# Order and rows of the matmuls in a chunked RWKV-7 recurrence inside a two-block kernel

## What is computed

```python
def rwkv7_recurrence(r, decay, k, v, a_vec, b_vec):
    """S_t = S_{t-1} diag(w_t) + (S_{t-1} a_t) b_t^T + v_t k_t^T ;  y_t = S_t r_t."""
    def step(state, inp):
        r_t, w_t, k_t, v_t, a_t, b_t = inp
        sa = jnp.einsum('bhvk,bhk->bhv', state, a_t)
        state = (state * w_t[:, :, None, :] + sa[..., None] * b_t[:, :, None, :]
                 + v_t[..., None] * k_t[:, :, None, :])
        return state, jnp.einsum('bhvk,bhk->bhv', state, r_t)
    ...
```

## Time and profile before

| what | value |
|---|---|
| median of three runs | 1117.88 us |
| lowest, highest | 1114.72, 1118.47 us |
| profiled execution, its own time | 1117.52 us |
| its span in the trace | 1115.7 us |
| PE busy | 1088.8 us (98% of the span) |
| DVE, ACT, POOL busy | 670.3, 448.1, 35.6 us |
| matmul records | 8212 |

### The profile page before, as it was taken

The page is one execution under the profiler, slowest core; times in us unless marked ns, Lnnn a source line. Parts: engine busy times, 40 slices in busy tenths (PEclk is TensorE's granted clock), DMA queues, the critical chain, the costliest instruction groups (busy, mean ns, idle before and its releaser), DMA issues.

```text
span 1115.7 us, 19112 instructions
## 1 busy us (share of the span) xinstructions
PE 1088.8 (98%) x8212; PEld 896.2 (80%) x8212; DVE 670.3 (60%) x848; ACT 448.1 (40%) x573; POOL 35.6 (3%) x29
## 2 busy tenths in 40 slices
PE   9999999999998999999999999999999999999997
PEld 8999998999987669999998999989899753434343
DVE  6488777789554666777775573277559552222123
ACT  6333334864522244333335332267584521211112
POOL 0000000000430000000003000000000000000000
PEclk9999999999978999999999999999999999999999
DMA  9977756354200248598873353332356979999994
GB/s 333 390 257 238 251 188 206 119 175 148 90 2 2 76 140 314 190 337 295 306 265 114 96 184 110 108 118 104 114 192 264 375 319 402 422 410 419 422 418 201
DMA packets 121012, 254.29 MB, mean 228 GB/s; under 512 B 6241, under 2 KB 91505, under 8 KB 109426
## 3 DMA queue, kind: packets, MB, share of 16 engines
q1 hardware_dynamic: 119890, 250.54, 61.6%
q10 hardware_dynamic: 1056, 2.79, 0.8%
HBM read 252.25 MB, written 1.06 MB: 227 GB/s over the span
## 4 chain that ended last, share of the span: by engine, by line
PE 89%; DVE 6%; ACT 4%; issue 1%; DMA 0%; SPq 0%; ACTq 0%; DVEq 0%
PE ps L825 53%; PE ps L772 33%; ACT arena L1563 2%; DVE ring_r L2130 1%; ACT arena_r L1563 1%; DVE ring_r L2263 1%; PE ps L1308 1%; DVE arena L2451 1%; DVE arena L2317 1%; DMA x<-in_x 0%; DVE arena L2332 0%; PE ps L793 0%; ACT gb_r L1563 0%; PE ps L1513 0%; PE ps L781 0%
## 5 line engine op out<-in xcount | busy, mean ns | idle before, releaser
L825 PE MATMUL ps<-hall_r,arena_r 128*128 128x256 f32 x1632 | 299.6, 281 | 0.0
L825 PE MATMUL ps<-arena_r 128*128 128x256 f32 (+1 forms) x1216 | 284.4, 323 | 0.0
L2130 DVE TENSOR_TENSOR ring_r<-ring,arena_r 128x2048 fp32r<-128x2048 f32 x88 | 203.1, 2312 | 109.1 <-ACT arena_r L1563 106.6
L825 PEld LDWEIGHTS ps<-hall_r,arena_r 128*128 128x128 f32 x1632 | 252.8, 188 | 1.2 <-issue 0.3
L1563 ACT ACTIVATE arena_r<-ring 128x2048 fp32r<-128x2048 f32 (+1 forms) x101 | 191.1, 1899 | 150.3 <-PE ps L825 139.9
L825 PE MATMUL ps<-hall_r,ring_r 128*128 128x256 f32 x816 | 227.9, 279 | 0.0
L825 PEld LDWEIGHTS ps<-arena_r 128*128 128x128 f32 x1216 | 202.7, 188 | 18.9 <-issue 0.7
L772 PE MATMUL ps<-arena 64*64 64x32 f32 (+7 forms) x1944 | 195.8, 331 | 11.2 <-ACT arena L1563 5.0
L1563 ACT ACTIVATE arena<-ps 128x512 f32<-128x512 f32 (+3 forms) x136 | 80.4, 605 | 312.6 <-PE ps L825 186.2
L772 PEld LDWEIGHTS ps<-arena 128*64 128x64 f32 (+3 forms) x1944 | 117.8, 154 | 71.1 <-issue 58.6
L825 PEld LDWEIGHTS ps<-hall_r,ring_r 128*128 128x128 f32 x816 | 154.9, 190 | 0.9
(11 more groups left out here) (273 smaller groups left out, 1137.8 us busy)
## 6 DMA issues: line engine op xcount, KB each, us to landing
ring<-in_w_in SPq DMA_DIRECT2D x35, 1024.0 KB, 5.2
arena<-in_w_exp_down SPq DMA_DIRECT2D x32, 1024.0 KB, 11.8
ring<-in_ffn_up SPq DMA_DIRECT2D x22, 1024.0 KB, 5.3
ring<-in_ffn_down SPq DMA_DIRECT2D x22, 1024.0 KB, 5.0
ring<-in_ffn_gate SPq DMA_DIRECT2D x21, 1024.0 KB, 5.7
arena<-in_w_mod SPq DMA_DIRECT2D x18, 1024.0 KB, 9.3
arena<-in_w_exp_up SPq DMA_DIRECT2D x16, 1024.0 KB, 14.5
ring<-in_w_exp_gate SPq DMA_DIRECT2D x16, 1024.0 KB, 11.4
```

Source lines behind the costliest of these rows:

```text
L825: m = pe.matmul(out_, w[i], h[j], start=start and i + j == 0, stop=stop and j == 1, skip_group_check=group)
L2130: tt(lo(n), slot(n), hi(n), ALU.subtract).then_inc(S("w_lo"), 1)
```

## The change

Before, all products of a chunk stood together behind the waits. Now those that need only v stand ahead of the waits, in functions of their own: the right side's (`rec_rhs_v`) for the next chunk behind y of this one, the state's (`rec_state_v`) between the right side and u, y's (`rec_y_v`) between u and the wait for its copy. The first right side stands behind `inv_sums(5)`, ahead of the head sums and of `inv_update(5)`. Every product that takes its rows from a chunk (all but those with the state) contracts over that chunk's 64 rows (`rec_rows(c)`), so that the zeros aren't needed: v is kept once (`v_t`, two copies in place of four multiplications), and `u_zero` goes. The products with the state keep their 128 rows. The state's sums move from bank 4 to bank 7. ACT copies the first right side ahead of the attention's output and root, and DVE scales the attention's output behind each chunk's state; it waits for the last of these before the means of y. `keep_running` is defined and not called.

```diff
@@ -174,10 +174,10 @@
                         "dve_mix": [("cum", 2), ("kk_raw", 4), ("bonus_prod", 1), ("kk_unit", 1), ("b_bar", 1), ("k_bar", 1),
-                        ("arz", 4), ("bonus_v", 1), ("q_ready", 1), ("v_tok", 4), ("gram_b_masked", 4),
+                        ("arz", 4), ("bonus_v", 1), ("q_ready", 1), ("v_tok", 2), ("gram_b_masked", 4),
                         ("kn", 1)],
             "pool_all": [("c_zero", 2), ("selectors", 2), ("reset_ones", 1), ("reset_mask", 1), ("inv_0", 4),
-                         ("level_a", 5), ("u_zero", 1), ("gates_biased", 4), ("w_zero", 1)],
+                         ("level_a", 5), ("gates_biased", 4), ("w_zero", 1)],
             "pool_rec": [("rec_masked", 3), ("x_zero", 1)],
                          ("logits_kept_a", 1), ("final_a", 1)],
@@ -429,7 +429,7 @@
         kk, sq, kf = tiles(13), tiles(14), tiles(15)
         arz = A(16, 4096).rearrange("p (q k c j n) -> p q k c j n", q=2, k=4, c=NCH, j=2)
         b_bar, k_bar, bonus = tiles(20), tiles(21), tiles(22)
-        vz = A(0, 2048).rearrange("p (q t n) -> p q t n", q=2, t=TT)
+        v_t = A(0).rearrange("p (t n) -> p t n", t=TT)
         b_tok = A(13).rearrange("p (t n) -> p t n", t=TT)
         k_tok = A(10).rearrange("p (t n) -> p t n", t=TT)
         ab_t, rb_t, ak_t, rk_t = (A(j).rearrange("p (i n) -> p i n", n=CH) for j in (6, 7, 8, 9))
@@ -744,9 +744,6 @@
             for level in range(3, 6):
                 level_mask(level)
 
-            pool.wait_ge(*W("inv_x", 5))
-            pool.memset(A(20, 2048), 0.0).then_inc(S("u_zero"), 1)
-
             pool.wait_ge(*W("mod_kept", 3))
             pool.wait_ge(*W("gate_bias", 64))
             for j in range(4):
@@ -1038,7 +1035,7 @@
             pe.wait_ge(*W("b_bar", 1))
             by_token(b_bar, 4, "b_turned")
             project(11, True)
-            pe.wait_ge(*W("v_tok", 4))
+            pe.wait_ge(*W("v_tok", 2))
             pe.wait_ge(*W("k_sq", 1))
             four(6, lambda o, k: mm(o, head_mean, sb_sq_k[:, k, :]), "k_ms")
             project(12, True)
@@ -1136,6 +1133,59 @@
                         else:
                             m = mm(out_, inv_x[half, i, :], blocks_of(inv_tt[half, i, :], level, 1))
                 m.then_inc(S("inv_t"), 1)
+
+            def rec_rows(c):
+                return slice((c % 2) * CH, (c % 2 + 1) * CH)
+
+            def rec_rhs_v(c):
+                for h in range(8):
+                    m = mm(ps[rec_rows(c), 0, h * CH:(h + 1) * CH], ak_t[rec_rows(c), 8 * (c // 2) + h, :],
+                           v_t[rec_rows(c), c // 2, h * HD:(h + 1) * HD], start=h == 0, stop=c == 0, group=True)
+                if c == 0:
+                    m.then_inc(S("rec_rhs"), 1)
+
+            def rec_rhs_state(c):
+                for h in range(8):
+                    m = mm(ps[rec_rows(c), 0, h * CH:(h + 1) * CH], arz[:, h % 2, h // 2, c, 0, :],
+                           state[:, c % 2, h // 2, :], start=False, group=True)
+                m.then_inc(S("rec_rhs"), 1)
+
+            def rec_state_v(c):
+                for h in range(8):
+                    o = ps[(h % 2) * HD:(h % 2 + 1) * HD, 7, (h // 2) * HD:(h // 2 + 1) * HD]
+                    mm(o, k_tok[rec_rows(c), c // 2, h * HD:(h + 1) * HD],
+                       v_t[rec_rows(c), c // 2, h * HD:(h + 1) * HD], start=h < 2, stop=False, group=True)
+
+            def rec_state_u(c):
+                for h in range(8):
+                    o = ps[(h % 2) * HD:(h % 2 + 1) * HD, 7, (h // 2) * HD:(h // 2 + 1) * HD]
+                    m = mm(o, b_tok[rec_rows(c), c // 2, h * HD:(h + 1) * HD],
+                           u_z[rec_rows(c), c % 2, h * HD:(h + 1) * HD], start=False, group=True)
+                m.then_inc(S("rec_state"), 1)
+
+            def rec_y_at(c, h):
+                return ps[(h % 2) * HD:(h % 2 + 1) * HD, 2 + c % 2, (h // 2) * CH:(h // 2 + 1) * CH]
+
+            def rec_y_v(c):
+                if c >= 2:
+                    pe.wait_ge(*W("y_kept", c - 1))
+                for h in range(8):
+                    mm(rec_y_at(c, h), v_t[rec_rows(c), c // 2, h * HD:(h + 1) * HD],
+                       rk_t[rec_rows(c), 8 * (c // 2) + h, :], start=h < 2, stop=False, group=True)
+
+            def rec_y_u(c):
+                for h in range(8):
+                    m = mm(rec_y_at(c, h), u_z[rec_rows(c), c % 2, h * HD:(h + 1) * HD],
+                           rb_t[rec_rows(c), 8 * (c // 2) + h, :], start=False, stop=c == 0, group=True)
+                if c:
+                    for h in range(8):
+                        m = mm(rec_y_at(c, h), state[:, c % 2, h // 2, :], arz[:, h % 2, h // 2, c, 1, :],
+                               start=False, group=True)
+                m.then_inc(S("rec_y"), 1)
+
+            def keep_running():
+                for i in range(2):
+                    mm(ps[:, 7, 0:256], zeros[:, 0:P], zeros)
 
             for p in range(4):
                 sb_scores(p)
@@ -1155,49 +1205,36 @@
             sb_values(1)
             inv_sums(5)
             pe.wait_ge(*W("sb_expo", 4))
+            pe.wait_ge(*W("rec_masked", 3))
+            rec_rhs_v(0)
             pe.wait_ge(*W("sbo_sq", 2))
             four(4, lambda o, k: mm(o, head_mean, sq[:, k, :]), "sbo_ms")
             inv_update(5)
 
 
-            pe.wait_ge(*W("rec_masked", 3))
             for c in range(NCH):
-                t, base = c // 2, (c % 2) * CH
-                rows_ = slice(base, base + CH)
-                pe.wait_ge(*W("tt_added", 5))
                 if c:
                     pe.wait_ge(*W("state", c))
-                for h in range(8):
-                    o = ps[rows_, 0, h * CH:(h + 1) * CH]
-                    if c:
-                        mm(o, arz[:, h % 2, h // 2, c, 0, :], state[:, c % 2, h // 2, :], stop=False)
-                    m = mm(o, ak_t[:, 8 * t + h, :], vz[:, c % 2, t, h * HD:(h + 1) * HD], start=c == 0)
-                m.then_inc(S("rec_rhs"), 1)
+                    rec_rhs_state(c)
+                if c < NCH - 1:
+                    rec_state_v(c)
+                if c == 0:
+                    pe.wait_ge(*W("sb_kept", 1))
+                    rec_y_v(c)
+                    pe.wait_ge(*W("tt_added", 5))
                 pe.wait_ge(*W("rhs_kept", c + 1))
                 for h in range(8):
-                    m = mm(ps[rows_, 1, h * CH:(h + 1) * CH], inv_tt[:, 8 * t + h, :],
-                           rhs_z[:, c % 2, h * HD:(h + 1) * HD])
+                    m = mm(ps[rec_rows(c), 1, h * CH:(h + 1) * CH], inv_tt[rec_rows(c), 8 * (c // 2) + h, :],
+                           rhs_z[rec_rows(c), c % 2, h * HD:(h + 1) * HD])
                 m.then_inc(S("rec_u"), 1)
+                if c:
+                    rec_y_v(c)
                 pe.wait_ge(*W("u_kept", c + 1))
-                if c == 0:
-                    pe.wait_ge(*W("sb_kept", 1))
-                    pe.wait_ge(*W("sbo_root", 1))
                 if c < NCH - 1:
-                    for h in range(8):
-                        o = ps[(h % 2) * HD:(h % 2 + 1) * HD, 4, (h // 2) * HD:(h // 2 + 1) * HD]
-                        mm(o, b_tok[:, t, h * HD:(h + 1) * HD], u_z[:, c % 2, h * HD:(h + 1) * HD], stop=False)
-                        m = mm(o, k_tok[:, t, h * HD:(h + 1) * HD], vz[:, c % 2, t, h * HD:(h + 1) * HD],
-                               start=False)
-                    m.then_inc(S("rec_state"), 1)
-                if c >= 2:
-                    pe.wait_ge(*W("y_kept", c - 1))
-                for h in range(8):
-                    o = ps[(h % 2) * HD:(h % 2 + 1) * HD, 2 + c % 2, (h // 2) * CH:(h // 2 + 1) * CH]
-                    if c:
-                        mm(o, state[:, c % 2, h // 2, :], arz[:, h % 2, h // 2, c, 1, :], stop=False)
-                    mm(o, u_z[:, c % 2, h * HD:(h + 1) * HD], rb_t[:, 8 * t + h, :], start=c == 0, stop=False)
-                    m = mm(o, vz[:, c % 2, t, h * HD:(h + 1) * HD], rk_t[:, 8 * t + h, :], start=False)
-                m.then_inc(S("rec_y"), 1)
+                    rec_state_u(c)
+                rec_y_u(c)
+                if c < NCH - 1:
+                    rec_rhs_v(c + 1)
             pe.wait_ge(*W("y_kept", 4))
             four(0, lambda o, k: mm(o, head_mean, y_rw[:, k, :]), "y_mean")
 
@@ -1824,15 +1861,14 @@
             square_out(0)
             square_out(1)
             keep_sums(5)
-            f(mix[0], banks(2), ACT.Copy).then_inc(S("sb_kept"), 1)
-            act.wait_ge(*W("sbo_ms", 2))
-            f(kn, banks(4), ACT.Sqrt, bias=EPS_COL).then_inc(S("sbo_root"), 1)
-
             for c in range(NCH):
                 rows_ = slice((c % 2) * CH, (c % 2 + 1) * CH)
                 act.wait_ge(*W("rec_rhs", c + 1))
-                act.wait_ge(*W("u_zero", 1))
                 f(rhs_z[rows_, c % 2, :], ps[rows_, 0, :], ACT.Copy).then_inc(S("rhs_kept"), 1)
+                if c == 0:
```

(15 more changed lines are left out.)

## The result

The changed kernel takes 1124.63 us (median of 6 runs, 1122.35 to 1125.06), the kernel before 1116.30 (6 runs, 1113.04 to 1118.63): ratio 1.0082, 95% interval 1.0066 to 1.0098. It is slower by 8.3 us where 7.4 us less had been forecast. The profiled execution has a span of 1122.9 us against 1115.7, and its own time is 1124.70.

A forecast was written before the change was run, and what follows sets the result against it. TensorE was taken to bound the kernel (busy 1088.8 of 1115.7 us, 89% of the chain). Terms +0.93 - 2.21 - 0.82 - 3.47 - 0.55 - 0.74 - 0.58 = -7.44, applied to the 1117.88 median, gave 1110.4 us; range 1107 to 1117.

The forecast's parts named there:

- the first rival: Recurrence: TensorE's clock still falls once, a 10.24 us stretch at 0.50 costing 3.9 us; 1114.3 us, chance 0.15.
- the whole sum: Inverse's end through recurrence: all gains and losses together, -7.44 us, with the recurrence at full clock.
- the period: Recurrence chunks 1 and 2, from u to u: 6.46 us against 7.01 and 7.20, saving 0.55 and 0.74.
- a fuller PE is safer: Recurrence clock: activity releases the throttle, so more work and fewer gaps on PE keep the clock up; no size given.
- the second rival: Clock stays at 0.50 for the whole recurrence because 64 rows count as less work: +5.3, 1123.2 us, chance 0.08.
- 7.44 + 0.90: Recurrence: forecast gain of 7.44 us, with the 0.90 taken off for eight shape changes added back.
- the third rival: Recurrence: column halves of 64-row tiles don't run side by side, +5.0, 1115.4 us, chance 0.07.
- a shape change: Recurrence, between 64 and 128 rows: bounded at 0.05 to 0.15 us, taken as 0.10, or 0.15 behind pairs.
- a product over 64 rows: Recurrence: should cost the same as over 128 rows with the same 64 columns, since loading weights sets the step.
- clock in before's recurrence: Old order at full clock would have lost 3.9 us, about half of the forecast gain.
- the gain arrives: Behind the recurrence all shifts earlier; the opposing rival, a later load or engine keeping its time: 1117.9 us, chance 0.08.
- What would show it: Signs: clock 1.00 through recurrence, idle between update and u under 0.1, period 6.4 to 6.5; wrong if clock is 0.50.

The follow-up runs named there:

- Experiment 2: Kernel before, old order on every engine, but products with v or u over 64 rows: 1131.20 us, ratio 1.0139.
- experiment 3: Changed kernel plus one idle product over 128 rows and 256 columns ahead of each of the four waits for u's copy: 1111.94 us, ratio 0.9966.
- experiment 5: Changed kernel plus four idle products, each over 64 rows and 64 columns of weights, ahead of the waits for u's copy: 1111.11 us, ratio 0.9963.
- 6: Changed kernel plus one idle 128-row product, in chunk 0 alone, ahead of the wait for u's copy: 1110.26 us, ratio 0.9961.
- 9: Changed kernel's new order with 64 rows in chunks 1 to 3 alone, 128 rows in chunk 0: 1110.49 us, ratio 0.9953.
- experiment 1: Changed kernel's new order, but all products over 128 rows with v padded by zeros as before: 1111.89 us, ratio 0.9963.
- 8: Changed kernel's new order with 64 rows in chunk 0 alone, 128 rows in chunks 1 to 3: 1111.41 us, ratio 0.9964.
- experiment 11: Changed kernel plus four idle 128-row products in the recurrence and five in the inverse: 1105.83 us, ratio 0.9913.
- 12: Changed kernel plus five idle 128-row products in the inverse alone: 1118.11 us, ratio 1.0021.
- 4: Kernel before with only the first right side moved ahead and DVE's scaling one place later, all 128 rows: 1113.52 us, ratio 0.9984.
- 13: Changed kernel plus 8 repeated projection products, meant to start the recurrence 0.9 us later: 1124.37 us, ratio 1.0083.
- 10: Kernel before plus five idle 128-row products in the inverse: 1111.78 us, ratio 0.9960.
- experiment 14: Changed kernel plus 17 repeated projection products, meant to start the recurrence 2.0 us later: 1124.27 us, ratio 1.0082.

## Why the prediction was wrong

- **The step that failed** is one sentence, by which the first rival was held off and the clock of the whole sum set: "But it stayed at 1.00 through 353.70 to 373.58 with idle gaps of 0.68 and 0.79 in each chunk, and the new stretch before 343.5 has 0.93 more work and no gap." The evidence was of products over 128 rows and was carried to products over 64, and so every term of the sum from u of chunk 0 on was priced at 1.00: the period was taken at 6.46 and measured 10.35 and 10.24, at 0.50. The rows had a warning: from 305.9 on the clock was at 0.50 with PE in `64*64` products and busy 12.78 of 13.7 us (though other `64*64` products, at 340.03 for one, ran at 1.00). I set that aside because its products had 32 moving elements and these have 64. Experiment 2 shows that 64 don't help, and the changed kernel has 34 us at 0.50 with PE busy in 97% of them.
- The Trainium skill (TensorE: Matmul & The Clock Gate, Part 1) says that "the default state is throttled, and activity releases the throttle"; I wrote that the rows agree that a fuller PE is safer. They don't: the changed kernel is fuller than the one before (idle 1.2 us of 34 against 4.9 of 20) and has the lower clock. Experiments 3, 5 and 6 agree with the rule in a weaker sense, since more work in the gaps did hold the clock up.
- **The chance of the second rival**, 0.08, was therefore far too small, and with it the range: 1124.63 lies above both 1117 and the rival's own 1123.2. The rival's mechanism was right. Its period was 10.3 and is 10.35 and 10.24. Its size at the means was too large (+5.3 for +2.8), as the clock fell at 347.2, not at 343.5, and chunk 0 had its u at the full clock; what it left out is that the low clock outlives the recurrence, +2.5 in the means and the out-projection, and that it comes again at 627, +1.5.
- **The prices were right,** for products at the full clock: order 8.34 against 7.44 + 0.90; period 6.51 against 6.46; column halves of 64-row tiles side by side (32 records of `64*64` in 1.61 us in 9, 32 of `128*64` in 1.61 in 1), so the third rival is out; a shape change 0.05 to 0.15; a product over 64 rows no cheaper than over 128; clock in before's recurrence 3.8 against 3.9. In 1, 3 and 9 the means start 7.3, 7.0 and 6.9 us earlier than in the profiled execution of before, and their spans, 1110.3, 1108.8 and 1108.8, are 5.4, 6.9 and 6.9 shorter (1 has a stretch of 3.4 us at 0.50 from 615.1 on): the gain arrives. Their medians, 1110.49 to 1111.94, are where the forecast was (1110.4).
- **A smaller flaw** is what the sum was made against. Of the 17 runs of before that stand beside experiments 8 to 11, ten lie at 1113.2 to 1115.0 and seven at 1117.0 to 1118.7; the profiled one (1117.52) is of the upper kind. The distance is about the 3.8 us of one low stretch. The runs' mean clock, 0.991 to 0.992 in the ten and 0.986 to 0.987 in the seven, differs by what 10.24 us at 0.50 take off a mean over 1115.7 (5.12 of them, 0.005). So many runs of before probably don't have the stretch, though there is no trace of such a run. If so, half of the sum, the 3.9 of clock, was there to be won in the upper runs alone, and against a median of the lower kind (1114.70) the new order wins only 3 to 4 us.
- "What would show it" was right as a test: the idle time between update and u is gone, and the granted clock of 0.50 in the recurrence was named as what would prove the forecast wrong.

**What is shown and what is not.** Shown: without the 64-row half of the change the recurrence is not slow (1 against the changed kernel), and with the old order that half is enough (2); it is not the order, not the shape changes (3 and 11 have more of them), not the clock of the inverse (12). Shown too: a small addition undoes it, 128 rows in chunk 0 or in the rest, or one idle product (6), though 5 and 6 still fall at the last chunk in some runs. Argued, not shown: that within that half it is the rows. Every kernel here with 128 rows in a chunk's own products also has POOL's memset and DVE's four instructions for v, and no run has 64 rows throughout and that work too. Against the padding work speak before and 4, which have the memset and fall all the same, 3 and 11, which don't and hold, and the second fall of 2. Open as well: the moment beyond the 0.94 us of 13, what the chip counts, and why so little tips it. I have no rule that says beforehand on which side of the edge such a kernel lies.

## What to carry to other kernels

Halving the rows of these small fp32 products won nothing (1.61 us for 32 records either way), cost 0.05 to 0.15 us at each change of shape, and went with half of TensorE's clock for 34 us. Ask of each stage of small products what the clock is, and count a stretch as safe only on rows with the same tiles. And where PE waits in such a stage, an idle product ahead of the wait is cheap to try: four took 12.7 us off the changed kernel, five in the inverse 6.1 more (1105.83 in experiment 11 against 1111.94 in 3, on another chip), and the new order over 128 rows with the five is 11.0 us under the kernel before (1105.29 against 1116.28 beside it). Look at all the runs when you try it: in 5, 6, 10 and 12 the runs of one kernel lie up to 5 to 11 us apart. And when work is added only to shift a later stage, read the shift from the trace: of the 2.0 us of experiment 14, 0.26 arrived.

## What the runs showed of the hardware

- TensorE at 0.50 for 34.13 us while it was busy for 32.97 of them; the clock came back 5.0 us after the products had turned from the recurrence's to `128*128` (376.34 to 381.35 in the changed kernel; 384.72 to 389.1, 4.4 us, in experiment 2).
- The same recurrence at 1.00 with 2.8 us of idle products added (experiment 3), and for most of it with four of 0.59 us in `64*64` tiles (experiment 5, 342.0 to 365.7).
- The same kernel with and without a low stretch: the 17 runs of before at two levels of mean clock, 0.991 to 0.992 and 0.986 to 0.987, 1113.2 to 1115.0 and 1117.0 to 1118.7.
- A fall 280 us away from the change: the changed kernel has 3.4 us at 0.50 at 627.1, with PE busy in all of it; experiment 1 has one at 615.1, and 2, 4, 5, 6 and 8 have one between 614 and 638; the kernel before and the other experiments have none.
